# A new order for the start of the attention stage: first scores before the fourth block's maxima, loads in order of need, sliding units regrouped

## What is computed

```
h    = RMSNorm(x) * (1 + scale(c)) + shift(c)
proj = h @ w_in                              # q,k,v,f,z of A | q,k,v,z of B | merge gates
A (8 heads of 64): logits = q.k/8 + F_t - F_s, causal; softmax; @ v; * SiLU(z); @ w_o_fox
B (8 heads, 2 kv heads, chunk-causal window of 128): logits = q.k/8 - slope*dist, with a sink
                   in the softmax; @ v; * SiLU(z); @ w_o_swa
m    = sigmoid(gA) * yA + sigmoid(gB) * yB
out  = x + gate(c) * (m @ w_out)
```

## Time and profile before

| | |
|---|---|
| time of before, median of 3 runs | 2127.08 us (2125.26 to 2133.05) |
| the profiled execution, its own time | 2127.95 us |
| span of the profiled execution, first to last instruction | 2126.2 us |
| mean granted TensorE clock | 0.962 |
| PE busy | 1979.7 us, 93% of the span |
| DVE, ACT, POOL busy | 885.6, 737.5, 550.5 us |
| attention stage in the trace | from about 1105 to 1722 us |

### The profile page before, as it was taken

The page is one execution under the profiler, slowest core; times in us unless marked ns, Lnnn a source line. Parts: engine busy times, 40 slices in busy tenths (PEclk is TensorE's granted clock), DMA queues, the critical chain, the costliest instruction groups (busy, mean ns, idle before and its releaser), DMA issues. The chain is left out here.

```text
span 2126.2 us, 27983 instructions
## 1 busy us (share of the span) xinstructions
PE 1979.7 (93%) x9722; PEld 1555.5 (73%) x9722; DVE 885.6 (42%) x1851; ACT 737.5 (35%) x1375; POOL 550.5 (26%) x502
## 2 busy tenths in 40 slices
PE   7389999999999999999989899999999959998998
PEld 2368778798788788888866566666666639997887
DVE  2945555562212220000234455555565335554332
ACT  2622222220112132121115677767777751002000
POOL 1600000000000000000004576767777742110000
PEclk9589999999999999999986999999999979999999
DMA  6233443345512212121424446446464334232322
GB/s 238 98 101 89 120 119 99 118 133 136 134 50 89 78 49 89 49 89 58 124 74 95 96 112 159 113 92 144 108 141 99 74 122 137 80 99 99 119 91 77
DMA packets 235435, 222.63 MB, mean 105 GB/s; under 512 B 54610, under 2 KB 188498, under 8 KB 234292
## 3 DMA queue, kind: packets, MB, share of 16 engines
q1 hardware_dynamic: 221892, 180.95, 30.8%
q0 software_dynamic: 11648, 39.85, 5.9%
q10 hardware_dynamic: 1792, 0.53, 0.1%
HBM read 149.18 MB, written 71.70 MB: 104 GB/s over the span
## 5 line engine op out<-in xcount | busy, mean ns | idle before, releaser
L1242 POOL TENSOR_TENSOR Pl<-PT,Ph 128x512 fp32r<-128x512 f32 (+2 forms) x350 | 415.5, 1204 | 200.2 <-ACT Ph L1342 192.9
L474 PE MATMUL pj<-hTh,Wh 128*128 128x512 f32 x768 | 299.6, 390 | 0.7 <-DVE Wl L679 0.4
L475 PE MATMUL pj<-hTl,Wh 128*128 128x512 f32 x768 | 299.0, 389 | 0.0
L476 PE MATMUL pj<-hTh,Wl 128*128 128x512 f32 x768 | 298.9, 389 | 0.0
L474 PE MATMUL pj<-Wh,hTh 128*128 128x512 f32 (+1 forms) x640 | 246.1, 385 | 23.9 <-DVE Wl L679 23.9
L376 POOL DMA_DIRECT2D wraw<-in_w_in x84 | 45.1, 537 | 856.4 <-DVE Wl L679 850.3
L1335 ACT ACTIVATE PT<-sc 128x512 f32<-128x512 f32 (+2 forms) x350 | 192.6, 550 | 137.7 <-PE sc L1267 46.2
L476 PE MATMUL pj<-Wh,hTl 128*128 128x512 f32 (+1 forms) x640 | 240.0, 375 | 0.0
L475 PE MATMUL pj<-Wl,hTh 128*128 128x512 f32 (+1 forms) x640 | 239.9, 375 | 0.0
L1342 ACT ACTIVATE Ph<-PT 128x512 fp32r<-128x512 f32 (+2 forms) x350 | 207.9, 594 | 11.2
L1082 DVE TENSOR_REDUCE part_max<-mx 128x1 f32<-128x512 f32 (+3 forms) x267 | 157.6, 599 | 98.4 <-PE mx L1028 97.1
(11 more groups left out here) (231 smaller groups left out, 3553.5 us busy)
## 6 DMA issues: line engine op xcount, KB each, us to landing
qk_scratch<-qThl SPq DMA_DIRECT2D x96, 256.0 KB, 2.8
wraw<-in_w_in POOLq DMA_DIRECT2D x88, 256.0 KB, 3.8
g_scratch<-st SPq DMA_DIRECT2D x64, 256.0 KB, 2.4
gt<-g_scratch SPq DMA_DIRECT2D x16, 1024.0 KB, 7.8
xin<-in_x POOLq DMA_DIRECT2D x16, 512.0 KB, 5.0
wada<-in_w_ada SPq DMA_DIRECT2D x8, 1024.0 KB, 7.7
z_scratch<-st SPq DMA_DIRECT2D x32, 256.0 KB, 2.4
Qb<-qk_scratch SPq DMA_DIRECT2D x32, 256.0 KB
```

Of the source, the lines that this page charges most:

```text
L474: nc.tensor.matmul(out, a_hi, b_hi, start=first, stop=False)
L475: nc.tensor.matmul(out, a_hi, b_lo, start=False, stop=False)
L476: return nc.tensor.matmul(out, a_lo, b_hi, start=False, stop=last)
L1242: pool.tensor_tensor(Pl[n % NPH][0:rows, 0:w], PT[n % NP][0:rows, 0:w], Ph[n % NPH][0:rows, 0:w].bitcast(F32), ALU.subtract).then_inc(low_ ...
```

## The change

Seven numbers or expressions change, all of them in the planner:

- in head 0 the four sliding units no longer stand one in block 2 and three in block 3, but all four in block 3;
- no maximum of the attention stage is placed before step 1 (it was -3), so the scores of steps 0 to 3 come first;
- the maxima of sliding tiles are due 11 steps ahead of their tile instead of 16, in all heads; for blocks it stays 16;
- the tables are written in steps 4 to 9 instead of 1 to 6, and the first sliding tile's maxima are due 8.5 steps after their start instead of 7.5;
- the first loads are issued in another order: block 3's queries first, the second half of block 2's and the sinks later, the first gates earlier, the next head's keys and the first two sliding tiles later.

```
@@ -817,7 +817,7 @@
-        units = ((0, 1, 1, 2) if i >= JB else (0, 0, 1, 3))[j]
+        units = ((0, 1, 1, 2) if i >= JB else (0, 0, 0, 4))[j]
@@ -864,15 +864,15 @@
-    TILE_LEAD, ROW_LAG, SPACING = 16, 3, {"f": 1.05, "s": 1.5}
-    TABLES_AT, TABLE_TURNS = 1, 6
+    TILE_LEAD, ROW_LAG, SPACING = {"f": 16, "s": 11}, 3, {"f": 1.05, "s": 1.5}
+    TABLES_AT, TABLE_TURNS = 4, 6
...
-            due = min(start - TILE_LEAD, due)
+            due = min(start - TILE_LEAD[kind], due)
             if (kind, i) == ("s", 0):
-                due = TABLES_AT + 7.5
+                due = TABLES_AT + 8.5
@@ -896,7 +896,7 @@
-    at = [None] * NU + [max(math.floor(due), START + u // 2) for u, (it, due) in enumerate(later)]
+    at = [None] * NU + [max(math.floor(due), 1 + u // 2) for u, (it, due) in enumerate(later)]
@@ -911,11 +911,11 @@
-    k_due: START + 2 + 2 * c if h < 2
+    k_due: START + 6 + c if h < 2
-    q_due: START + i - NE + 1 if i < NQ
+    q_due: START + 8 * (i - NE) if i < NQ
-    s_due: START + 1 + 7 * t if t < 2
+    s_due: START + 4 + 11 * t if t < 2
-    z_due: START + 2 + 2 * e if e < NZ
+    z_due: START + 1 + e if e < NZ
@@ -1192,9 +1192,9 @@
-                    if n == START:
+                    if n == START + 1:
                         load_q(sp, NE - 1, (1,))
-                    if n == START + 1:
+                    if n == START + 3:
                         sp.dma_start(sinks[:], io["swa_sinks"].to_broadcast([P, SWA_H])).then_inc(sinks_in, 16)
```

More of the change, by code:

```diff
@@ L913, in attention @@
     row_step = lambda kind, i: at[row_item(kind, i)]
-    k_due = when(((h, c), START + 2 + 2 * c if h < 2 else last["f", (h - 2) * JB + 3] - AHEAD + 1 + 5 * c) for h in range(1, FOX_H) for c in range(JB))
-    q_due = when((i, START + i - NE + 1 if i < NQ else last["f", i - NQ] - AHEAD + 1) for i in range(NE, NB))
+    k_due = when(((h, c), START + 6 + c if h < 2 else last["f", (h - 2) * JB + 3] - AHEAD + 1 + 5 * c) for h in range(1, FOX_H) for c in range(JB))
+    q_due = when((i, START + 8 * (i - NE) if i < NQ else last["f", i - NQ] - AHEAD + 1) for i in range(NE, NB))
     v_due = when(((h, c), values_read[h * JB - 1, c]) for h in range(1, FOX_H) for c in range(JB))
-    s_due = when((t, START + 1 + 7 * t if t < 2 else last["s", 2 * t - 3] + 1) for t in range(TT))
-    z_due = when((e, START + 2 + 2 * e if e < NZ else last[blocks[e - NZ]] + 2) for e in range(NBLK))
+    s_due = when((t, START + 4 + 11 * t if t < 2 else last["s", 2 * t - 3] + 1) for t in range(TT))
+    z_due = when((e, START + 1 + e if e < NZ else last[blocks[e - NZ]] + 2) for e in range(NBLK))
     row_move = when(((kind, i), row_step(kind, i) + 1) for kind, m, n in (("f", NE, NB), ("s", 0, TT)) for i in range(m, n))
```

## The result

The changed kernel is slower by 3.0%, where the forecast was no difference: 2194.09 us (median of 4 runs, 2189.69 to 2198.92) against 2130.07 us for the kernel before on the same chip. The ratio is 1.0296, with a 95% interval of 1.0251 to 1.034. The profiled execution of the changed kernel took 2198.92 us, with a span of 2197.3 us.

A forecast was written before the change was run, and what follows sets the result against it. PE, busy 93% of the span, was taken to bound the kernel through its waits and clock. Head 0's 18.6 us gain less 13.4 us lost in other heads took 2127.95 to 2122.7 us; 8-in-10 range 2104 to 2137.

The forecast's parts named there:

- The row landing: Moved rows before each sliding tile's scores: land in 1.9 us, no wait; other end 1.0 us in each of 15 tiles.
- The waits for Ka: Next head's first maximum, six places: waits lengthen by 7.4 us in all, five becoming 1.7 to 2.4 us long.
- Dips: Half-clock stretches of some 3 us behind four of six Ka waits, 1.5 us lost each, 6 us taken.
- Head 0: First head of the attention stage: 95.2 us instead of 113.8, 18.6 us gained.
- the wait for biasB: Head 0, PE's wait for the tables on ACT: the 3.2 us go entirely.
- The wait for tile 2's load: Head 0, sliding tile 2: PE waits 2.5 us instead of 6.2; 2 to 3.5 us would show it right.
- PE's step 41: End of head 0: done by about 1197 us; before 1190 or after 1205 us would show the forecast wrong.
- The clock: Head 0's half-clock loss: 4.1 us at the start, 1.5 behind an ACT wait, 2.8 behind tile 2's load, instead of 18.9.
- DVE's set-up: Start of head 0: waits for the sinks, done at about 1114 us, costing PE 0.5 us at most.
- Row coincidence: Other heads, tile 3's and block 8's rows four steps apart instead of one: no difference, -9 to +7 us over seven heads.
- The one that ended slower: Rival: half-clock stretches of 26.0 us behind waits of 1.7 to 2.8 us; 2154 us with three, chance 0.12.
- A wait of a sliding score for shift_rows DMAs: Sign of being wrong: PE waiting for moved rows before a sliding tile's score, where no wait was forecast.

The follow-up runs named there:

- row_sooner: Changed kernel with the transposed row and move of each sliding tile two steps earlier, maxima unmoved; 2153.7 us, 1.0115 of before.
- ka_sooner_alone: Changed kernel with only the loads of the next head's keys issued every fourth step instead of every fifth; 2176.5 us, 1.0218 of before.
- ka_sooner: row_sooner with the loads of the next head's keys issued every fourth step instead of every fifth; 2131.1 us, 0.9996 of before.
- before_ka_sooner: Kernel before with only the next head's key loads issued every fourth step instead of every fifth; 2118.0 us, 0.9939 of before.
- spread_ka_sooner: setup_spread with the loads of the next head's keys issued every fourth step instead of every fifth; 2114.1 us, 0.9932 of before.
- setup_spread: tile2_row with DVE's set-up behind the first distance table cut into pieces behind its reads of steps 1, 2 and 3; 2129.1 us, 1.0002 of before.
- The lead of 13: Changed kernel with sliding tiles' lead 13 steps from tile 3 on, tiles 0 to 2 keeping 11; 2154.3 us, 1.0114 of before.
- tile2_row: lead16_from3 with tile 2's row and its move two steps sooner; 2124.2 us, 0.9958 of before.
- lead16_from3: Changed kernel with sliding tiles' lead back at 16 steps from tile 3 on, tiles 0 to 2 keeping 11; 2129.0 us, 0.9987 of before.
- light_loads: Changed kernel with smaller bulk loads from head 1 or 2 and sliding tile 4 on, output wrong, issues and waits kept; 2140.4 us, 1.0037 of before.

## Why the prediction was wrong

**The row landing: the step that failed.** The prediction took 2.9 us of slack between the last issue and the score, and a landing of 1.9 us, "and no wait; the other end is 1.0 us in each of 15 tiles". The slack was about right: 2.4 or 3.5 us. The landing was 5.6 to 7.2 us instead of 1.9, and beyond the 3.9 us that was to be the upper end. Both rows are medians of DMAs that lie elsewhere in SP's list; most of the moved rows are issued just when SP issues keys, values and queries for the next block. The trace of before showed how busy that is, in a window just there (share 0.93):

```profile
1210.00:1220.00 10.00, 8.35 (x46) 5.94 (x45) 5.78 (x14) 8.22 (x16) 6.76 (x7) 1.00 0.93 221
```

The upper end should have been made from a landing among such loads, and the earlier trace rows had one: 4.4 us from the end of the issue for block 3's Qb. Even that would have given 1.5 us in each of 15 tiles, 22 us, and not the 33.7 us of waits that came. Price with the half clock: 40.4 us by row_sooner.

The Trainium skill's fixed cost of 2.0 us was cited as speaking for no wait. The section gives it for DMAs that GpSimd issues, while these go over ACT's queue. Where little else was under way the traces don't contradict it, since the rows had landed within 2.25 us; under load the measured value is about three times as large. The error was to take the figure of a quiet queue for a busy one, and the agreement with the 1.9 us row was with the wrong row.

**The waits for Ka: right mechanism.** Predicted: five places, 1.7 to 2.4 us each, and 7.4 us more than before. Measured: 12.0 us in five, of 2.0 to 2.8 us, with a sixth of 2.4 us put down to shift_rows at the same matmul, so 14.4 us where before had 3.8, 10.6 more. Dips were expected behind four of the six and stand behind five. The predicted price of what the change added was 13.4 us. The runs price all that these waits cost: 17.6 us by ka_sooner_alone and 22.6 by ka_sooner, and 12 us in before itself by before_ka_sooner. The difference, 5 to 10 us, is what the change added.

**Head 0: 7.8 us gained in the profiled execution, not 18.6.** The start does what it should: PE's first score is at 1104.57 us, at once behind the stage's start, and the wait for biasB has shrunk to 0.5 us. The wait for tile 2's load is 3.4 us (predicted 2.5, range 2 to 3.5). PE's step 41 ends at 1206.7 us (predicted 1197; "wrong after 1205"). The waits went from 21.6 to 15.3 us, 6.3 less where 8.1 less were predicted. The clock is where the sum failed: the prediction had half clock outside waits fall from 41.1 us to some 18, a gain of 10.5 us, and it came to 38: 6.1 us at the start (9.0 predicted), 4.9 behind the wait for DVE, the 10.2 and the 17.1 of the windows above. The gain was some 1.5 us. Part of this is luck of the execution, as the four kernels with the same head 0 show (92.6 to 103.1 us); against the two with the old start (105.0 and 109.4) they are 9 us shorter on average.

Within that, "0.5 us at most" for DVE's set-up was 3.6 us. The set-up was costed from when the sinks land. Its own length grew, by 2.8 us up to the end of its last memset:

```profile
1107.77 0.90 DVE L1390 CAST R<-R 128x128 f32<-128x128 int32 x1
1108.71 0.23 DVE L1391 TENSOR_SCALAR R<-R 128x128 f32<-128x128 f32 x1
1108.97 1.25 DVE L1392 TENSOR_TENSOR R<-R 128x128 f32<-128x128 f32 x1
...
1110.90 1.22 DVE L1391 TENSOR_SCALAR R<-R 64x64 f32<-64x64 f32 x1
```

```profile
1107.31 1.28 POOL L1242 TENSOR_TENSOR Pl<-PT,Ph 128x512 fp32r<-128x512 f32 x1 [2.28 <-ACT Ph L1342]
1108.80 3.27 POOL L1242 TENSOR_TENSOR Pl<-PT,Ph 128x512 fp32r<-128x512 f32 x3 [0.20 <-ACT Ph L1342]
```

The same three instructions took 0.23, 0.29 and 0.19 us before, when POOL's first low half only came at 1115.15 us:

```profile
1108.69 0.23 DVE L1390 CAST R<-R 128x128 f32<-128x128 int32 x1
...
1109.21 0.29 DVE L1392 TENSOR_TENSOR R<-R 128x128 f32<-128x128 f32 x1
...
1110.05 0.19 DVE L1391 TENSOR_SCALAR R<-R 64x64 f32<-64x64 f32 x1
```

The early scores started POOL early, and DVE's set-up, which ran beside POOL for the first time, was slowed. All three traces with the old start have the short times; the eleven with the new start and the set-up in one piece (or with only its last memset moved) all have several long ones. In spread_ka_sooner, where these instructions stand some 4 us later and mostly between POOL's, they take 0.19 to 0.29 us again; in setup_spread one of the six is long (0.83). No run keeps POOL away and nothing else, so POOL as the cause is the likely reading, not a tested one. The prediction moved PE's work and looked at who waits for it, not at what the woken engine does to its neighbour.

**Row coincidence.** Predicted no difference, -9 to +7 us. POOL's and DVE's waits went from 16.8 to 19.5 us in all; right for this kernel, and 2.4 of the 2.7 us more stand where a wait for Ka does. The lead of 13, with some 8 us in its six waits, shows what can hang on it.

**The rivals.** The one that ended slower named half clock, which is over a third of the loss (30 of 82 us), but by another cause. It asked for long stretches behind waits of 1.7 to 2.8 us. What came behind head 0 were sixteen short ones, none over 6.8 us; six stood beside waits of over 4 us, which no rival had. "A wait of a sliding score for shift_rows DMAs" stood among the signs of being wrong, with no rival and no price of its own. It was bounded at 15 us and came to 40.

## What to carry to other kernels

When a step is moved closer to its reader, price the DMA in between by a landing at the same place in the other queues' lists, and where the trace hides it (it was early enough before), take the slowest landing among bulk loads as the upper end, not the nearest one in bytes. A wait of 2 us on the bounding engine should be charged for its clock as well: here 0.46 us for each us of work at half clock, in stretches of 3.4 to 6.8 us, which added some 30 us to 47 us of waits. And when an engine is started earlier, list what else runs in the new overlap.

## What the runs showed of the hardware

- A 4 KB move between two places of SBUF, issued on ACT's queue, landed 5.6 to 7.2 us behind its issue in nine tiles, with the DMA engines at a share of 0.73 to 1.11, and after 4.0 us in a tenth. With lighter loads it landed after 2.8 to 4.0 us in five tiles and within 2.3 us in five others; in the changed kernel itself within 2.25 us in tile 14, at a share of 0.29.
- The half clock. In the changed kernel 14 of the 15 waits of 2.0 us or more behind head 0 have a stretch at half clock beside them; in the waits of over 4 us the clock falls while PE still waits (at 1301.9 us in a wait that ends at 1304.75). Short waits for Ka are not safe: in tile2_row one of 1.24 us was followed by 10.2 us at half clock (below), in lead16_from3 one of 0.58 us by 3.4. The waits for POOL, up to 0.7 us and 24 to 27 in each kernel, had such a stretch begin within 1.5 us of their end at most twice in any kernel. Nor is the length of a stretch set by the wait. The wait for biasB, 3.2 us in before and 3.1 in before_ka_sooner at the same place, was followed by 26 us in the one and 10 us in the other; the wait for tile 2's load, 3.2 to 3.8 us, by 17.1, 17.1, 17.1 and 6.8 us in the four kernels with the same head 0. Over all kernels with the new start it was 1.8 to 3.8 us, and the stretch at it 3.4 us (row_sooner) to 30.7 us (light_loads). What sets it stayed open. It goes with the spread between runs of one kernel (before: 2118 to 2146 us, those that take longer at a lower mean clock).

  From tile2_row, a row of PE's timeline and the window of the clock behind it:

```profile
1306.19 0.30 PE L1028 MATMUL mx<-Ka,Qa 66*128 66x128 f32 x1 [1.24 <-DMA Ka<-qk_scratch]
```

```profile
1306.80:1316.90 10.10, 10.10 (x26) 6.46 (x26) 4.25 (x14) 4.39 (x8) 3.41 (x4) 0.50 0.56 118
```

- DVE's CAST, TENSOR_SCALAR and TENSOR_TENSOR on SBUF took 0.7 to 1.3 us in many cases instead of 0.2 to 0.3 beside POOL's TENSOR_TENSOR of 1.27 us, while its MEMSET of 1.76 us stayed as it was. No run was made for this alone. The Trainium skill ("Trainium Architecture — The Big Picture", "What this means for kernel authors") names a pair of ports that these two engines share under an exclusive lock, which fits.
